# Eight more matmuls ahead of each feed-forward loop of a two-block transformer kernel

## What is computed

```python
D_MODEL, SEQ, DEPTH, D_FF = 1024, 256, 2, 2816

def swiglu(x, w_in, w_out):
    a, b = jnp.split(x @ w_in, 2, axis=-1)
    return (jax.nn.silu(a) * b) @ w_out

for l in range(DEPTH):                                  # block 1; block 2 alike
    x = x + 0.5 * swiglu(rmsnorm(x, ffn1_norm[l]), w_ffn1_in[l], w_ffn1_out[l])
    x = x + mixer(rmsnorm(x, mix_norm[l]))              # attention, recurrences, gates
    x = x + 0.5 * swiglu(rmsnorm(x, ffn2_norm[l]), w_ffn2_in[l], w_ffn2_out[l])
```

## Time and profile before

| what | value |
|---|---|
| three runs | 2398.32, 2409.42, 2410.43 us; median 2409.42 us |
| the profiled execution | 2425.61 us, its span 2423.8 us |
| mean granted TensorE clock | 0.999 of full speed |
| busy, share of the span | PE 99%, PEld 97%, DVE 65%, ACT 49%, POOL 5% |
| DMA | 406.77 MB, mean 168 GB/s |

### The profile page before, as it was taken

How to read it: one execution, slowest core, us unless ns; L and a number is a source line. 1 busy time by engine, 2 the same in 40 slices (tenths; PEclk the granted TensorE clock), 3 DMA queues, 4 the chain that set the end, 5 groups by cost and what they waited for, 6 DMA issues and landing times.

```text
span 2423.8 us, 52429 instructions
## 1 busy us (share of the span) xinstructions
PE 2399.4 (99%) x23054; PEld 2346.3 (97%) x23054; DVE 1585.5 (65%) x1430; ACT 1196.2 (49%) x1207; POOL 116.6 (5%) x74
## 2 busy tenths in 40 slices
PE   9999999999999999999999999999999999999998
PEld 8999999999999999999999999998999999999998
DVE  6656777765575568777556655866656656857554
ACT  5545655544353456565344444835445444735433
POOL 0000151000000002500000000000000000000000
PEclk9999999999999999999999999999999999999999
DMA  8555454555555554445555555513655665514552
GB/s 287 190 186 173 130 169 140 175 191 183 182 177 186 191 176 148 143 139 181 184 190 171 176 190 180 159 55 108 206 190 174 203 196 165 174 38 136 193 177 102
DMA packets 322772, 406.77 MB, mean 168 GB/s; under 512 B 6480, under 2 KB 291152, under 8 KB 322384
## 3 DMA queue, kind: packets, MB, share of 16 engines
q1 hardware_dynamic: 321488, 400.58, 51.3%
q10 hardware_dynamic: 1152, 4.22, 0.5%
HBM read 403.72 MB, written 1.05 MB: 167 GB/s over the span
## 4 chain that ended last, share of the span: by engine, by line
PE 93%; DVE 4%; ACT 2%; issue 1%; DMA 0%; SPq 0%; DVEq 0%; ACTq 0%
PE ps L339 84%; PE ps L344 8%; DVE w_lo L303 1%; ACT w_hi L298 1%; ACT x_hl L366 1%; DVE sq L401 1%; DMA raw<-in_w_ffn_in 0%; DVE x_hl L391 0%; PE ps L1481 0%; PE ps L2197 0%; ACT sq L370 0%; DVE x L2185 0%; DVE x L623 0%; ACT k_t L1126 0%; DVE m_lo L1248 0%
## 5 line engine op out<-in xcount | busy, mean ns | idle before, releaser
L339 PE MATMUL ps<-x_hl,w_hi 128*128 128x256 f32 x7808 | 1376.2, 280 | 5.5 <-DVE x_hl L391 2.9
L303 DVE TENSOR_TENSOR w_lo<-raw,w_hi 128x2048 fp32r<-128x2048 f32 x383 | 881.7, 2303 | 495.7 <-ACT w_hi L298 495.0
L339 PEld LDWEIGHTS ps<-x_hl,w_hi 128*128 128x128 f32 x7808 | 1191.4, 189 | 12.4 <-issue 9.3
L339 PE MATMUL ps<-x_hl,w_lo 128*128 128x256 f32 x3904 | 1090.1, 279 | 0.0
L298 ACT CAST w_hi<-raw 128x2048 fp32r<-128x2048 f32 x383 | 730.2, 1908 | 641.1 <-PE ps L339 635.9
L339 PEld LDWEIGHTS ps<-x_hl,w_lo 128*128 128x128 f32 x3904 | 733.3, 188 | 0.0
L339 PE MATMUL ps<-h_hi,w_hi 128*128 128x256 f32 x1408 | 393.9, 280 | 0.0
L339 PE MATMUL ps<-h_lo,w_hi 128*128 128x256 f32 x1408 | 393.9, 280 | 0.0
L339 PE MATMUL ps<-h_hi,w_lo 128*128 128x256 f32 x1408 | 393.9, 280 | 0.0
L339 PEld LDWEIGHTS ps<-h_hi,w_hi 128*128 128x128 f32 x1408 | 268.8, 191 | 0.0
L339 PEld LDWEIGHTS ps<-h_hi,w_lo 128*128 128x128 f32 x1408 | 264.3, 188 | 0.0
(11 more groups left out here) (456 smaller groups left out, 2498.8 us busy)
## 6 DMA issues: line engine op xcount, KB each, us to landing
raw<-in_w_ffn_in SPq DMA_DIRECT2D x87, 1024.0 KB, 5.1
raw<-in_w_in SPq DMA_DIRECT2D x74, 1024.0 KB, 5.4
raw<-in_w_ffn_out SPq DMA_DIRECT2D x44, 1024.0 KB, 4.9
raw<-in_ffn_w_gate SPq DMA_DIRECT2D x44, 1024.0 KB, 5.3
raw<-in_ffn_w_up SPq DMA_DIRECT2D x44, 1024.0 KB, 5.3
raw<-in_ffn_w_down SPq DMA_DIRECT2D x44, 1024.0 KB, 4.8
raw<-in_w_out SPq DMA_DIRECT2D x16, 1024.0 KB, 5.1
raw<-in_w_mem_kv SPq DMA_DIRECT2D x8, 1024.0 KB, 5.1
```

What stands on the lines that cost most here:

```text
L303: nc.vector.tensor_tensor(w_lo[:, slot, :], raw[:, slot, :], w_hi[:, slot, :].bitcast(F32), ALU.subtract).then_inc(lo_ready, 1)
L339: mm = nc.tensor.matmul(out_ap, l, r, start=first and n == 0, stop=last and n == 2, skip_group_check=True)
```

## The change

Between the wait for `var_ready` and the matmul of zeros over bank 3, each FFN gets eight matmuls. For chunks 0 to 3 of x there is one of 512 columns (weights: the first 128 columns of the chunk's low part; moving: the chunk's high and low part) and one of 256 columns (weights: the other 128 columns of the low part; moving: the high part). All overwrite bank 3, which the matmul of zeros behind them overwrites again, so the values that the kernel computes stay the same.

```diff
             hidden(q, 1, 6)
             pe.wait_ge(var_ready, n + 1)
+            for k in range(4):
+                mm(ps[:, 3, :], x_lo[:, k, 0:P], x_hl[:, k, :, :], True, False)
+                mm(ps[:, 3, 0:T], x_lo[:, k, P:T], x_hi[:, k, :], True, False)
             mm(ps[:, 3, :], zero_w[:, :], zeros, True, False)
             with pe.Fori(1, FP - 1) as i:
```

## The result

The changed kernel takes 2442.64 us, median of four runs (2438.93 to 2447.54), against 2409.93 us (2398.32 to 2417.32) for the kernel before beside it. The ratio is 1.0134 with a 95% interval of 1.0089 to 1.0178: **1.3% slower**, where 0.56% faster was forecast as the likeliest. The time lies above the stated range, which ended at 2440. It is 5.8 us under Rival 2 (2448.4 us).

What follows compares the result with a forecast made beforehand. The prediction took TensorE, busy 99%, alone to set the time. From the profiled 2425.6 us, +9.6 us for the added matmuls and -39.2 us for six slow loops turned fast gave 2396.0 us; range 2386 to 2440 us.

Steps and rivals of the forecast that it cites:

- Rival 2: FFN loops: each pair's 256-column matmul fixes the slow pace in all loops, costing 13.2 us, to 2448.4 us; chance 0.24.
- What bounds the kernel: Whole kernel: TensorE, busy 99% of the span at its top clock of 2.4 GHz, alone sets the time.
- two paces: FFN loops: the same code runs at 117.8 or 113.3 ns a matmul, six loops slow and two fast.
- what a loop is worth: Each FFN loop of 1488 matmuls: the slow or fast pace makes a difference of 6.6 us.
- Where the pace is set: Loop entry: pace decided as matmuls restart behind the zeros, there by the second triple; what comes right before may matter.
- The cost: Eight added matmuls ahead of the zeros: 1.39 us per FFN (1.37 to 1.41), plain cost +9.6 us in all.
- The idle 1.12 us of stage 0: First FFN: TensorE's wait for `ta`, which the added work would fill, along with 0.23 us for `hid`.
- the 0.14 of stage 6: Stage 6, start of the second unit: a wait of 0.14 us that the added work would remove.
- The effect on the pace: FFN loops: between 39.2 us gained if all end fast and 13.2 us lost if all slow; fast end taken.
- the mixer's 512-column stretch: Mixers of block 1: wide matmuls came out of a slow stream, with fast triples behind; taken as nearest row.
- Rival 1: FFN loops: the added work changes no pace, leaving the bare cost, 2419.0 us (2410 to 2428); chance 0.34.
- The base: Profiled execution, 2425.61 us: its 16.2 us over the median was read as a per-loop pace lottery, not profiler cost.

Runs made afterwards that it cites:

- e13: Kernel before plus two 512/256-column pairs per FFN behind the matmul of zeros, into bank 4, right before the loop: 2414.01 us, ratio 0.9996.
- e6: The changed kernel with each of the four pairs turned round, 256 columns first and 512 second: 2399.44 us, ratio 0.9944 to the kernel before.
- e9: The changed kernel with one more 512-column matmul behind the four pairs, ahead of the zeros: 2395.34 us, ratio 0.9952 to the kernel before.
- e12: Kernel before plus three matmuls per FFN, of 512, 256 and 512 columns, ahead of the zeros: 2387.35 us, ratio 0.9883.
- e11: The changed kernel once more, unedited, profiled and timed: 2446.44 us, ratio 1.0127 to the kernel before.
- e10: The changed kernel with eight 256-column matmuls in place of the four pairs, none of 512: 2435.26 us, ratio 1.0136 to the kernel before.
- e8: Kernel before plus one 256-column fp32r matmul alone per FFN ahead of the zeros: 2409.32 us, ratio 1.0035.
- e7: Kernel before plus one 512-column fp32r matmul alone per FFN ahead of the zeros: 2416.19 us, ratio 1.0042.
- e4: The changed kernel with its four pairs moved behind the zeros, into bank 4, right before the loop: 2394.38 us, ratio 0.9931 to the kernel before.

## Why the prediction was wrong

- **What bounds the kernel, two paces, what a loop is worth: right.** 163.22 and 169.62 us are found again to the hundredth, and e13's steps are the 6.6 us.
- **Where the pace is set: right in the main.** In the seven stages other than stage 0 it is set where the matmuls restart in front of the loop, by what comes before. In stage 0 a delay behind the entry, of 22 ns in the changed kernel, still turned it.
- **The cost: right, at its upper end.** The eight take 1.41 us per FFN (1.39 put, 1.37 to 1.41 bounded), since the four 512-column matmuls are 233 to 241 ns long, 236 on average, and not 231 (and the four of 256 columns 118, not 115.5). The idle 1.12 us of stage 0 and the 0.14 of stage 6 are gone, and of the 0.23 us 22 ns are left at most. The prediction's estimate by the Trainium skill (TensorE: Matmul & The Clock Gate, section Back-to-back issue gap), 1.30 us per FFN, is too low for this type: 1.41 was measured. The section gives its formula for an isolated matmul and other figures for a stream, so "the page knows one pace only" read it too narrowly.
- **The effect on the pace: the step that failed.** The text took the mixer's 512-column stretch for the nearest row and wrote "Wide fp32r matmuls have there led from slow to fast both times. That ... is why I take the fast end." The row was true and the analogy bad. That stretch ends in 512-column matmuls, with 32 small ones and no zeros behind them; the change's pairs end in one of 256 ahead of the zeros. In the place where the change puts them, the end tells the pace: with three or more added matmuls, a 512 at the end made the loop start fast in 24 of 24 loops (e6, e9, e12), and a 256 at the end slow in 24 of 24 (the change, e11, e10), stage 0 counted in, whatever unit stood ahead, all in the profiled executions. So the added work sets the pace, and it set the slow one: in place of the text's -39.2 us for six loops made fast, the paces of the loops added 6.2 us in the changed kernel's profiled execution (two loops 6.4 us slower each, stage 0 6.6 us faster) and 13.2 us in e11's (no fast loop against two). Rival 2 had said it: "The 256-column matmul of each pair restores the stream that is slow in six loops of eight". It got 0.24. Looking back, the last thing added was a nearer row than the widest thing added; but one 256 or one 512 alone fixes nothing (e8, e7), and behind the zeros four pairs that end in a 256 make loops fast (e4), so the width of the last matmul is no rule by itself. Nor do these runs part the width of the end from its operands or from the length of the whole sequence.
- **Rival 1, no change of pace: refuted** by fourteen slow of fourteen. What ran before a stream does change the stream's pace, by 4.4 ns a matmul, for 1488 matmuls on end. With this falls what the prediction concluded from the Trainium skill (TensorE: Matmul & The Clock Gate, section Step-by-step: what each phase is for), that a matmul's width before could not change the pace after. What the page itself says, that loading weights takes no read bandwidth from the running matmul, no run here tests.
- **The base: right in kind.** The spread of the kernel before is the draw of paces, not the profiler. It made the loss in the median larger than Rival 2's 13.2 us suggest: by the sum four loops or so are lost, not two.
- **The sizes.** Rival 2's 2448.4 against 2442.64 measured: the four runs lie at 2438.9, 2440.0, 2445.3 and 2447.5, the one at 2440.0 has a fast stage 0 (-6.6), and the median falls between the pairs; the base was 1.8 us too high there. The range stopped at 2440 by counting on a loop or two that would come out fast under Rival 2; since the sequence fixes seven, there were one or none. A case of 0.24 should have been wholly inside.

What stays open is the cause in the hardware. The runs show that a running fp32r stream has two lasting paces, that one matmul ahead of the zeros hands the pace on, and that three, eight or nine there set it. Two matmuls there, four to seven, or three in another order were not run. What is in step or out of step with what, they don't show, nor why one pair behind the zeros makes loops slow and four make them fast.

## What to carry to other kernels

Divide long stretches of the chain of waits by their count of matmuls before trusting "99% busy": two paces of one loop, and run times that differ in steps of one loop's difference, mean that the pace is set at the loop's entry. It can then be set on purpose by a few matmuls there that cost far less than a slow loop gains by turning fast (here three, 0.6 us, for 6.6). But which few has to be tried: their order, end, number and place all changed the outcome here. And a short wait behind the entry can undo it. When a change is bounded by an analogy to another stretch, compare first what touches the stream in question: the last matmuls and what stands between them and the stream.

## What was not expected of the hardware

- One 512-column fp32r matmul more per FFN takes the kernel from 2442.64 or 2446.44 to 2395.34 us.
- The paces are steady to 0.1 ns: 340.0 ns and 353.4 ns for three matmuls of 256 columns (163.22 and 169.62 us over 480 triples), at the same granted clock 1.00, across all kernels and both blocks.
- A delay of 22 ns at one matmul turned a running loop from slow to fast in stage 0 of the changed kernel, worth 6.6 us.
- The last 512-column matmul ahead of the zeros tells the pace at which the loop starts by its length, some 240 ns (fast) or 233 (slow), in e6, e7, e9 and e12. The faster loop follows the longer matmul.
- Six bfloat16 matmuls of zeros, 1.3 us of other work, turned the pace over in six of seven stages instead of resetting it.
